# The first panel behind three norms: multiplied with scaled columns, its outputs corrected afterwards

## What is computed

```python
for l in range(DEPTH):                                   # DEPTH = 2
    mod = cond @ w_ada[l] + b_ada[l]
    sh1, sc1, g1, sh2, sc2, g2 = split(mod, 6)
    h = x * (1.0 + sc1) + sh1
    y = token_mixer(h, ...)                              # begins with h @ w_in[l], ends with @ w_out
    x = layer_norm(ALPHA * x + g1 * y, ln1_g[l], ln1_b[l])      # norm "mix"
    h = x * (1.0 + sc2) + sh2
    y = conv_ffn(h, ...)                                 # begins with h @ w_up[l], ends with @ w_down
    x = layer_norm(ALPHA * x + g2 * y, ln2_g[l], ln2_b[l])      # norm "ffn"
```

## Time and profile before

| | us |
|---|---|
| median of 3 runs (lowest, highest) | 3418.07 (3417.81, 3419.47) |
| the profiled run, time | 3417.27 |
| its span in the profile | 3415.5 |
| PE busy | 3297.4, 97% of the span |
| DVE busy | 2102.7, 62% |
| ACT busy | 1321.9, 39% |
| POOL busy | 615.9, 18% |

### The profile page before, as it was taken

The page is one execution under the profiler, slowest core; times in us unless marked ns, Lnnn a source line. Parts: engine busy times, 40 slices in busy tenths (PEclk is TensorE's granted clock), DMA queues, the critical chain, the costliest instruction groups (busy, mean ns, idle before and its releaser), DMA issues. The chain is left out here.

```text
span 3415.5 us, 39169 instructions
## 1 busy us (share of the span) xinstructions
PE 3297.4 (97%) x15472; PEld 2651.3 (78%) x15472; DVE 2102.7 (62%) x2693; ACT 1321.9 (39%) x1720; POOL 615.9 (18%) x496
## 2 busy tenths in 40 slices
PE   8899999999999999999999999999999999999998
PEld 6577788886677788877788777888777887778886
DVE  8854576548753666447866746554677666465545
ACT  4664322234663322234333234343444332343323
POOL 2222232131212222111000232000210001320002
PEclk9999999999999999999999999999999999999999
DMA  3122454322122544332212232222221212222222
GB/s 131 43 64 81 176 199 189 128 93 78 38 76 88 197 189 189 107 121 74 74 62 67 88 105 88 99 99 99 74 87 63 74 59 92 96 87 92 94 98 74
DMA packets 72183, 344.47 MB, mean 101 GB/s; under 512 B 25152, under 2 KB 26048, under 8 KB 35648
## 3 DMA queue, kind: packets, MB, share of 16 engines
q1 hardware_dynamic: 70416, 339.12, 28.8%
q0 software_dynamic: 576, 2.33, 0.2%
q10 hardware_dynamic: 1008, 0.51, 0.1%
HBM read 340.51 MB, written 2.10 MB: 100 GB/s over the span
## 5 line engine op out<-in xcount | busy, mean ns | idle before, releaser
L901 PE MATMUL bank<-Hhi_b,whi_b 128*128 128x512 f32 x2976 | 1205.4, 405 | 42.9 <-ACT Hhi_b L1282 15.5
L902 PE MATMUL bank<-Hhi_b,wlo_b 128*128 128x512 f32 x2976 | 1164.6, 391 | 0.0
L908 PE MATMUL bank<-Hlo_b,whi_b 128*128 128x512 f32 x2976 | 1156.9, 392 | 1.1 <-DVE Hlo_b L2336 0.9
L879 DVE TENSOR_TENSOR wlo_b<-raw_b,whi_b 128x2048 fp32r<-128x2048 f32 (+2 forms) x290 | 624.5, 2153 | 460.8 <-ACT whi_b L873 460.8
L901 PEld LDWEIGHTS bank<-Hhi_b,whi_b 128*128 128x128 f32 x2976 | 562.4, 189 | 186.7 <-issue 30.9
L908 PEld LDWEIGHTS bank<-Hlo_b,whi_b 128*128 128x128 f32 x2976 | 561.2, 189 | 123.0 <-DVE Hlo_b L2336 3.8
L902 PEld LDWEIGHTS bank<-Hhi_b,wlo_b 128*128 128x128 f32 x2976 | 562.4, 189 | 120.1 <-issue 9.1
L873 ACT ACTIVATE whi_b<-raw_b 128x2048 fp32r<-128x2048 f32 (+2 forms) x290 | 511.8, 1765 | 365.0 <-PE bank L908 361.4
L901 PE MATMUL bank<-Uhi_b,whi_b 128*128 128x512 f32 x1024 | 404.9, 395 | 3.7 <-POOL Ulo_b L990 3.7
L902 PE MATMUL bank<-Uhi_b,wlo_b 128*128 128x512 f32 x1024 | 399.8, 390 | 0.0
L908 PE MATMUL bank<-Ulo_b,whi_b 128*128 128x512 f32 x1024 | 386.2, 390 | 0.0
(11 more groups left out here) (253 smaller groups left out, 3397.2 us busy)
## 6 DMA issues: line engine op xcount, KB each, us to landing
raw_b<-in_w SPq DMA_DIRECT2D x234, 1024.0 KB, 4.8
ada_b<-in_wada SPq DMA_DIRECT2D x48, 1024.0 KB, 6.9
raw_b<-in_w SPq DMA_DIRECT2D x40, 512.0 KB, 3.7
raw_b<-in_w SPq DMA_DIRECT2D x16, 768.0 KB, 4.3
rel_b<-in_rel SPq DMA_DIRECT2D x128, 24.0 KB, 2.4
X_keep<-in_x SPq DMA_DIRECT2D x4, 512.0 KB, 9.5
decay_b<-in_decay POOLq DMA_DIRECT2D x2, 1024.0 KB, 6.8
out<-X_keep SPq DMA_DIRECT2D x8, 256.0 KB, 2.0
```

The costliest lines, as they stand in the source:

```text
L879: self.nc.vector.tensor_tensor(self.wlo[n % RAW_SLOTS][:, 0:words], self.raw[n % RAW_SLOTS][:, 0:words], self.whi[n % HI_SLOTS][:, 0:words ...
L901: self.nc.tensor.matmul(out, whi[:, k, cols], xhi, start=(k == 0), stop=False)
L902: self.nc.tensor.matmul(out, wlo[:, k, cols], xhi, start=False, stop=False)
L908: mm = self.nc.tensor.matmul(out, whi[:, k, cols], xlo, start=False, stop=(k == nk - 1))
```

## The change

For the three norms in `FOLDED` the first panel behind the norm is no longer multiplied with the normalised columns. With gain a and shift b per feature, h = (x − mean)·r·a + b, and so W·h = r·(W·(a·x) − mean·(W·a)) + W·b. 

- Item "scaled": ACT writes a·x into Hhi (Copy with a scale), DVE the rest into Hlo. Columns 0, 1, 4 stand behind output 4's items, columns 2, 3, 5 behind output 5's, then 6 and 7 behind their own.
- The round of the first panel moves from output 6's items to output 5's, ahead of scaled 2, 3, 5; its rest moves behind them.
- In "lnend" PE first makes W·a and W·b (`column_sums`: 32 matmuls with 4 columns each) and then the panel's 48 matmuls, in three groups between the sums and the two spreads. The round of the second panel now stands ahead of "lnend", its rest behind it, ahead of "lnx".
- The normalised columns are still made ("lnx", "lnlo"), into the same Hhi and Hlo as soon as the scaled ones have been read. The second panel uses them and takes them one after another.
- Behind the second panel "unfold" corrects the two outputs of the first: a small reduction, two operations on DVE and one on ACT for each output. Only then the outputs are read as before. In layer 1 this second panel has no gaps any more, so no convolution taps stand in it.
- The first output lies in a small bank, the second in a wide one. At the start, 12 tiny DVE instructions make the coefficients in split form.

```diff
@@ ffn_stages
+            ahead = halfway is not None and u0 + j == 0
-            s.product(n, 8, 256, [(i, ("fg", l, c)) for i, c in enumerate(cs)], ("H", l, "ffn"), k_outer=(u0 + j == 0))
+            if not ahead:
+                s.product(n, 8, 256, [(i, ("fg", l, c)) for i, c in enumerate(cs)], ("H", l, "ffn"),
+                          k_outer=(u0 + j == 0))
...
+            if not ahead:
+                gates()
...
-            s.product(n, 8, 256, [(i, ("fu", l, c)) for i, c in enumerate(cs)], ("H", l, "ffn"))
+            s.product(n, 8, 256, [(i, ("fu", l, c)) for i, c in enumerate(cs)], ("H", l, "ffn"), k_outer=ahead)
             n += 1
             between()
+            if ahead:
+                norm_outputs(s, l, "mix")
+                gates()
@@ ln_column
+    folded = (l, w) in FOLDED
     if c == 5:
         s.add("lnshift", l, w, 6)
         s.add("lnshift", l, w, 7)
-    if c == 6:
+        if folded:
+            s.round_next()
+    if folded:
+        for i in {4: (0, 1, 4), 5: (2, 3, 5), 6: (6,), 7: (7,)}.get(c, ()):
+            s.add("scaled", l, w, i)
+        if c == 5:
+            s.rest_next()
+    elif c == 6:
         s.split_ahead(n)
@@ layer_norm_stages
+    after, jobs = FOLDED[l, w]
+    s.load_ahead(n)
+    s.wide.take(jobs[1])
+    s.last_use[n] = jobs[1]
+    s.round_next()
+    s.add("lnend", l, w, n)
+    s.rest_next()
     for k in range(DC):
-        if after:
-            s.temp("hf", 2, ("hf", *after, k))
+        s.temp("hf", 2, ("hf", *after, k))
         s.add("lnx", l, w, k, after)
@@ act_work
+            elif kind == "scaled":
+                act.wait_ge(*after("xc", l, w, c))
+                act_e.activation(k.Hhi[:, c], X[:, c], ACT.Copy, scale=normed(l, w, 0, c))
+            elif kind == "unfold":
+                act.wait_ge(*after("rooted", *job))
+                act_e.activation(z, z, ACT.Identity, bias=wsum[:, i, 1:2])
@@ dve_work
+            elif kind == "scaled":
+                dve.wait_ge(*after("sc hi", l, w, c))
+                nv.scalar_tensor_tensor(out=k.Hlo[:, c], in0=X[:, c], scalar=normed(l, w, 0, c),
+                                        in1=k.Hhi[:, c].bitcast(F32), op0=ALU.mult, op1=ALU.subtract)
+            elif kind == "unfold":
...
+                nv.scalar_tensor_tensor(out=buf(u), in0=msb[:], scalar=wsum[:, i, 0:1], in1=z, op0=ALU.mult,
+                                        op1=ALU.subtract)
+                nv.scalar_tensor_tensor(out=z, in0=buf(u), scalar=-1.0, in1=k.out_of(("br", l, w))[:], op0=ALU.mult,
+                                        op1=ALU.mult)
@@ pe_work, "lnend"
+                if n is not None:
+                    column_sums(pe, l, w, n)
                 pe.wait_ge(*after("xc", l, w, 7))
                 sum_by_tile(mn, X[:, 7], False, True).then_inc(*mark("pe", mn))
...
+                    scaled_products(pe, l, w, n, FOLD_ORDER[0:1])
                 spread(("bm", l, w), few_mean).then_inc(*mark("pe", ("bm", l, w)))
+                    scaled_products(pe, l, w, n, FOLD_ORDER[1:3])
                 spread(("br", l, w), few_var).then_inc(*mark("pe", ("br", l, w)))
+                    scaled_products(pe, l, w, n, FOLD_ORDER[3:])
```

More of the change, by code:

```diff
@@ L690, in schedule_two @@
                 cols, rhs, nk, then = [(j, ("yp", l, a, b + j)) for j in range(2)], ("Y", l, MIX_FROM[a]), 4, mixed
-            if i == 0:
+            if i == 0 and l > 0:
+                lead_then = [(job, then) for _, job in cols]
+            elif i == 0 or i == 1 and l > 0:
                 s.product(n, nk, 256, cols, rhs, k_outer=True)
+                if i == 1:
+                    norm_outputs(s, l - 1, "ffn")
+                    for job, lead in lead_then:
+                        lead(job)
                 for _, job in cols:
@@ L724, in gathered @@
         s.small.take(("ss", l, w))
+        if (l, w) in FOLDED:
+            s.small.take(("sw", l, w))
+            s.small.take(FOLDED[l, w][1][0])
         s.small.take(("bm", l, w))
@@ L755, in ln_column, with layer_norm_stages, norm_outputs @@
         s.add("lnshift", l, w, 7)
-    if c == 6:
-        s.split_ahead(n)
-def layer_norm_stages(s, l, w, after):
-    s.add("lnend", l, w)
-    if after:
-        s.round_next()
+        if folded:
[6 more added lines that the diff above has]
+    elif c == 6:
+        s.split_ahead(n)
+FOLDED = {(0, "mix"): ((0, "ffn"), (("fg", 0, 0), ("fg", 0, 1))),
+          (0, "ffn"): ((1, "mix"), (("z", 1, "ca", 0), ("z", 1, "cb", 0))),
+          (1, "mix"): ((1, "ffn"), (("fg", 1, 0), ("fg", 1, 1)))}
+FOLD_ORDER = (0, 1, 4, 2, 3, 5, 6, 7)
+def layer_norm_stages(s, n, l, w):
+    if (l, w) not in FOLDED:
+        s.add("lnend", l, w, None)
+        for k in range(DC):
+            s.add("lnx", l, w, k, None)
+        return
+    after, jobs = FOLDED[l, w]
[5 more added lines that the diff above has]
+    s.rest_next()
     for k in range(DC):
-        if after:
-            s.temp("hf", 2, ("hf", *after, k))
+        s.temp("hf", 2, ("hf", *after, k))
         s.add("lnx", l, w, k, after)
-        if after and k > 0:
+        if k > 0:
             s.add("lnlo", *after, k - 1)
-    if after:
-        s.add("lnlo", *after, DC - 1)
-        s.rest_next()
+    s.add("lnlo", *after, DC - 1)
+def norm_outputs(s, l, w):
+    for i in range(2):
+        s.temp("hf", 2, ("hf", "norm", l, w, i))
+        s.add("unfold", l, w, i)
 def psum_banks(nc):
@@ L1950, in act_work @@
                 z, job = k.out_of(("z", l, t, i))[:], ("z", l, t, i)
-                act.wait_ge(*after(*job))
+                act.wait_ge(*after(*(("normed", *job) if job in FOLDED[0, "ffn"][1] else job)))
                 if t == "ca":
@@ L2065, in act_work @@
                 if to:
+                    act.wait_ge(*after("sc free", l, w, c))
                     act_e.activation(k.Hhi[:, c], X[:, c], ACT.Identity, bias=normed(l, w, 1, c),
@@ L2077, in act_work @@
                 job, dst, ch = (("fg", l, c), ("fa", l, c), c) if kind == "evfg" else (("fu", l, c), ("fw", l, c), 22 + c)
-                act.wait_ge(*after(*job))
+                act.wait_ge(*after(*(("normed", *job) if job in FOLDED[l, "mix"][1] else job)))
                 reuse(act, dst)
@@ L2112, in dve_work @@
                     nv.tensor_tensor(coef[:, j, 1], coef[:, j, 1], shift, ALU.add).then_inc(*mark("dve", ("coef", j, 4)))
+                    dve.wait_ge(*after("coef", j, 0))
+                    dve.wait_ge(*after("coef", j, 4))
+                    for v in range(2):
+                        nv.tensor_copy(few_coef[:, j, :, 2 * v], coef[:, j, v]).then_inc(*mark("dve", ("few hi", j, v)))
+                    for v in range(2):
+                        dve.wait_ge(*after("few hi", j, v))
+                        nv.tensor_tensor(few_coef[:, j, :, 2 * v + 1], coef[:, j, v],
+                                         few_coef[:, j, :, 2 * v].bitcast(F32), ALU.subtract)\
+                            .then_inc(*mark("dve", ("few", j, v)))
                 build_tables(nc, dve, None, steps, "tab2", pos_i[:], invt[:, 0:1], [t[:] for t in tab_tmp], cos[:], sin[:],
@@ L2330, in dve_work @@
                 dve.wait_ge(*after("xm", l, w, c))
-                names = [("xr", l, w, c)] + ([("free", ("br", l, w))] if c == DC - 1 else [])
+                names = [("xr", l, w, c)] + ([("free", ("br", l, w))] if c == DC - 1 and not to else [])
                 nv.tensor_tensor(X[:, c], X[:, c], k.out_of(("br", l, w))[:], ALU.mult).then_inc(*mark("dve", *names))
@@ L2373, in spread, with column_sums, scaled_products @@
         return mm
+    def column_sums(pe, l, w, n):
+        j, sw, (whi, wlo) = NORMS[l, w][0], ("sw", l, w), k.weights(n, 256)
+        pe.wait_ge(*after("whi", n))
+        pe.wait_ge(*after("wlo", n))
+        reuse(pe, sw)
+        for v in range(2):
+            pe.wait_ge(*after("few", j, v))
+        for i in range(2):
+            cols, out = slice(i * P, (i + 1) * P), k.out_of(sw)[:, 4 * i:4 * i + 4]
+            for c in range(DC):
+                nt.matmul(out, whi[:, c, cols], few_coef[:, j, c], start=(c == 0), stop=False)
+                mm = nt.matmul(out, wlo[:, c, cols], few_coef[:, j, c], start=False, stop=(c == DC - 1))
+        mm.then_inc(*mark("pe", sw))
+    def scaled_products(pe, l, w, n, columns):
+        jobs, (whi, wlo) = FOLDED[l, w][1], k.weights(n, 256)
+        for c in columns:
+            first, last = c == FOLD_ORDER[0], c == FOLD_ORDER[-1]
+            pe.wait_ge(*after("sc", l, w, c))
+            for i, job in enumerate(jobs):
+                if first:
+                    reuse(pe, job)
+                out, cols = k.out_of(job)[:], slice(i * P, (i + 1) * P)
+                nt.matmul(out, whi[:, c, cols], k.Hhi[:, c], start=first, stop=False)
+                nt.matmul(out, wlo[:, c, cols], k.Hhi[:, c], start=False, stop=False)
+                mm = nt.matmul(out, whi[:, c, cols], k.Hlo[:, c], start=False, stop=last)
```

(3 more changed lines are left out.)

59 lines of the change are left out of this document (48 added, 11 removed).

## The result

The changed kernel takes 3471.63 us (median of 4 runs, 3467.38 to 3475.82); the kernel before, 3417.94 (4 runs, 3413.54 to 3419.47). The ratio is 1.0154, 95% interval 1.0141 to 1.0166: 53.7 us slower, where the prediction had 35 and a range that ends at 3470. The profiled run took 3471.97 with a span of 3469.9.

What follows compares the result with a forecast made beforehand. PE, busy 97% of the span, was taken as the bound. Norms at +10.4, +8.0 and +8.8 us make 27.2, plus 7.8 for the clock: +35.0, forecast 3453 us, range 3420 to 3470.

Steps and rivals of the forecast that it cites:

- Both standstills: PE idle 4 to 5 us ahead of column 6's sums, and 7 to 9 us ahead of the third panel.
- the walk: First norm followed through the engines' queues: column 6 ready at 2080.8, PE still from 2112.6 to 2122.0; +10.4 us.
- the clock's term: Lower clock after PE's waits: 1.6 us behind each third-panel standstill, 1 ahead of each norm; +7.8 us.
- The setup: 12 tiny instructions at the start: below 2 us on an engine with idle time, nothing taken; 2 if uncovered.
- a sign against it: A stretch far from the norms growing by over 3 us would show the forecast wrong.
- Rival C: Heavier: slow clock through the column sums, port conflicts, or late gate outputs delaying later panels; 3466 to 3480; 12%.
- The high end of the forecast: Column sums and the tail at half clock, 15.6 us in place of 3.0: +47.6 us, 3466.
- port term: At the scaled columns' rests, the port DVE and POOL share costs 5 us more per norm: +15, 3468.
- The gain of 5 us per norm: From stage end to second panel, PE's own work takes 17.6 us instead of 22.6 if nothing else moved.
- rival A: Faster: DVE and ACT keep up, column 6 not late, bank free during the second panel; 3403; 11%.
- The standstill for the bank: Ahead of the third panel PE waits for the second gate output's wide bank, 2112.6 to 2122.0 at the first norm.

Runs made afterwards that it cites:

- filled kernel: Against the changed kernel: idle matmuls in PE's standstills, sized to end before the standstill does; 3458.9 us.
- e1: Against the changed kernel: the 12 tiny coefficient instructions moved from the setup to a later item of layer 0; 3468.8 us.
- e9: Against e5_order2: 28 of the 32 column sums of each norm left out, results wrong, time alone counts; 3428.9 us.
- e5_order2: Against e4: scaled columns further back, 0, 1 behind output 5, 4, 2, 3 behind 6, 5 to 7 behind 7, round at output 5; 3431.2 us.
- e3: Against the changed kernel: second panel's two outputs in small banks, reduction of the column sums moved to the norm; 3464.9 us.
- e4: Against the changed kernel: edits of e1, e2 and e3 together, fourth panel's weights split ahead of the gate outputs; 3451.1 us.
- e2: Against the changed kernel: scaled columns 2, 3, 5 and the rest of the first panel's weights moved behind output 6's items; 3465.5 us.

## Why the prediction was right or wrong

- **Sign and mechanism** held. Both standstills are where the walk put them: column 6 ready at 2088.9 (walk 2080.8, plus the 7.3 us of offset: 2088.1), no wait ahead of a normalised column, 9.73 us ahead of the third panel (walk 9.4), released by DVE's taps, 6.99 and ACT's sigmoid behind the second norm. Two of the three waits ahead of the norm, 2.1 us for POOL's sums, the walk didn't have. Column 7's addition came 8.5 us later and not 5.5.
- **The step that failed is the clock's term.** It took 2.6 us per norm, 1.0 ahead and 1.6 behind. At the first norm, ahead, the tail lost 1.8 (nine matmuls at 0.43 and not 0.23), the scaled column ahead of the mean's spread 1.3 (six in 2.73 and not 1.4), sums and column sums about 1; behind, the third panel lost 2.5 (its matmuls are 0.43 apart from 2133.89 to 2139.14). That is 6.6, 4.0 more than taken. The slow matmuls of 128x512 alone lost 5.8, 4.9 and 5.7 us at the three norms; with the sums, an estimate of 11 us more than the 7.8 taken, and the norms grew 12.8 beyond the forecast. The prediction argued that DVE's delay of column 7 would hide the slow clock ahead of the norm. It did the reverse: column 7 waited 2.04 us for PE's slow tail. The filled kernel gave 9.9 back although the clock fell once more in it.
- **The setup** was the second term: taken at nothing, "2 if that cover is gone". It cost about 3: no idle time covered it, since DVE's tables, ACT's sines and PE's next panel follow each other there, and the delay brought two steps beside POOL. This was also the stretch far from the norms that the prediction named as a sign against it. Without it (e1) the median is 3468.8, just inside the range.
- **Rival C** had a slow clock through the column sums. They ran mostly at full clock, 0.11 apart, 3.9 us, near the 3.6 taken; what was slow lay around them. The high end of the forecast, 47.6 us, had them slow too, so that it agrees with the 47.8 of the norms is luck. (The floor of the Trainium skill, "TensorE: Matmul & The Clock Gate", section "Back-to-back issue gap", would give 0.8, an estimate without the weight loads, and the section itself says that its formula leaves these out at few columns; the measurement agrees with the price of the weight load.) Rival C's port term was too large: six rests beside POOL took 6.7 us where the walk had 5.7. The walk's reason for a small price, the rows' median, was weak all the same: a rest that met POOL took up to 1.78, and only three of six met it for long.
- **The gain of 5 us per norm** on PE was put down as real once the queues keep up (rival A, 3403). The order can be mended without taking work away, which the prediction didn't see, and then 40 of the 54 us are gone. But e9 shows that even without most of the column sums the time stays above the kernel before. ACT and DVE are 39% and 62% busy over the span, but in e5_order2 DVE is busy for 11.7 of the 12 us from 2070 to 2082, and ACT for 10.8 of those from 2094 to 2106.
- The standstill for the bank was one of two. The prediction's walk ended at the first bank; with it gone (e3) the next panel's weights were as late.
- The first block's 3.6 us have no term in the prediction; how much of them is scatter isn't known.

## To carry to other kernels

Work that is ready early should still stand behind whatever the next statistics wait for: the scaled columns put ahead of two additions held up two engines and lowered the clock, and the same operations put behind them gave back 20 of the 33 us that were left in e4. Follow also what the moved work then stands beside: the split that e2 moved beside POOL's sum made that sum 2.1 us longer, on the path. Price a standstill of PE of some microseconds with the slow matmuls behind it, here about 4 us behind the one ahead of the norm and 2.5 behind the other. And before moving PE's work off a wait, follow the engines that made the wait through the next three panels: their queues don't get shorter.

## What was not expected of the hardware

- A DVE operation with one input of 128x512 on f32 took 1.40 us beside POOL and 0.43 without it, in a stretch where 1.7 us of delay decided between the two. It goes the other way too: a POOL sum of 1.27 us took 3.40 where it started together with a DVE split of 2.28.
- Thirty-two weight loads and matmuls with 4 columns ran 0.11 us apart at full clock and 0.21 at the lower one. Where PE had stood still or run fillers before them, the clock fell in or behind them; where a full-speed stream stood before them (e5_order2), it stayed at 2.4 GHz.
- A plain f32 matmul of 128x512 took 0.9 us, four of the fp32r ones.
